# First 128 tokens ranked and gathered ahead; expert 0 begins without gates and list; first refill in halves; odd gathers around down

## Chip, cores and metric

One core of a Trainium2 chip. The metric is the device time of one execution in microseconds (us); the median of three runs of the kernel before is 1189.14 us (1188.91 to 1189.64).

## What is computed

One decoder layer in float32 for 256 tokens (S) of width 1024 (D). A front part makes one projection of x, sparse attention and a convolution branch, mixes them and adds the residual: `x1 = LayerNorm(alpha * x + mix)`. The mixture of experts follows: `logits = x1 @ w_router + b_router`, the top 4 of 32 experts per token, a softmax over the four as gates, and for each expert `act = (u + 1) * (g * sigmoid(1.702 g))` with clamped `g, u = t @ w_gate_up[e] + b_gate_up[e]`, then `out += gate * (act @ w_down[e] + b_down[e])`. A tail computes `LayerNorm(h + sigmoid(h @ W_pg) * (p @ W_pp))`.

## The kernel before

**Tiling.** Tokens stand in two blocks t of 128 (NT = 2). An expert takes its tokens in slots of CAP = 64: a one-hot matrix `sel` (token by slot, for two experts q = 0, 1 at once) gathers the rows of x1 by matmul into `XT` (8 blocks k of 128 features). `mask` says which expert a token picked (`pick`, L1546), a matmul with `upper` and `ones` counts the tokens ahead (L841 to L843), `slot1` (L1588) is the slot number, `one_hot` (L460) compares it with a ramp. Experts with more than 64 tokens take a second round: `wide` (L1596, L1600) holds that flag, which every engine loads into a register before it branches (`read_flag`, L506). Tokens beyond 128 of one expert go on a list (`need`, `place`, `more`; L861, L871), worked off behind expert 31.

**Weights.** Each expert needs six loads of 2 MB (`load_pair`, L336; CPE = 6): four for gate and up (w_gu), two for down (w_dn). There are ES = 11 places. Loads 0 to 10 are issued during the front part; from load 11 on (L560) SyncE waits until TensorE has used what lay in the place (`chunk_used`, `gu_done`, `d_done`; `pair_read`, L339) and issues the next. SyncE issues in order; transfers queue behind one another.

**An expert in one round** (`one_round`, L986) on TensorE: turn the gates by slot (`turn_gates`, L381), 32 gate-up products (L389, in two passes each, so 64 records in the trace), two turns of the result (L396), the flag, `before(e)`: the output of the expert ahead is spread to the tokens by `combine` (L409), then in odd experts the gather for the next two (L376), then down (16 products, 32 records). `use_down` (L914) waits for `t_read`, which VectorE sets when it has read both halves of the turned up-part (second L435 in `swiglu`), and for `act_ready` (L453), half by half. ScalarE evacuates the sums (L1261), the down rows (L1264) and the gathered rows (`xt_out`, L496). Expert 0 also turns the bias rows (L967), waits for ScalarE's copy (L1272) and combines them before down.

**The stretch around the change** (215 to 265 us). TensorE interleaves the last mixing products (L791) with turns of the residual (L801) and the router (L809); four short matmuls (`keep_clock`, L831) fill waits. VectorE: residual and statistics, `scale` (L1531) and `shift` (L1543) of each half row of x1, `pick(0)`, later `pick(1)`, slots of both blocks, one-hot of both, the last half of x1, the flags, the gates (L1602 to L1608), gates by slot (L472), `place`. Then TensorE gathers with both blocks, ScalarE evacuates XT, and expert 0 starts. GpSimd (POOL) has nothing to do between its bias work (L626) and two memsets (L629, L630), behind which SyncE loads the bias rows of down (L556).

## Time and profile before

| | |
|---|---|
| median of 3 runs | 1189.14 us |
| the profiled execution, its own time | 1189.43 us |
| its span, first to last instruction | 1187.7 us |
| TensorE busy | 1151.7 us (97%) |
| VectorE, ScalarE, GpSimd busy | 297.9, 172.5, 11.4 us |
| DMA moved | 448.16 MB |
| expert 0's first product starts | 239.09 us |
| experts end, tail begins | 1149.9 us |

An engine's busy time is the union of its instructions. L389 is line 389 of the kernel; helpers give all their instructions one line, so a product of any expert is L389. Times below are from the start of the span; the profiled execution takes 1.7 us more than its span.

### The profile page before, as it was taken

The numbers are of one execution on the slowest core, as the hardware profiler recorded it, in microseconds if no ns is written. First come the engines' busy times: TensorE is split into PE (matmuls) and PEld (weight loads), VectorE is DVE, ScalarE is ACT, GpSimd is POOL, SyncE is SP. The second block draws the span as 40 slices with busy tenths as digits, with TensorE's granted clock in tenths as the row PEclk, the third lists the DMA queues.
The fourth block names the chain that finished last, engine by engine and source line by source line (L and its number), as shares of the span: only waits on it lengthen the run. The fifth ranks groups of instructions, "written<-read, shape, count | busy, mean of one in ns | idle before, by whom it ended". The sixth has DMA issues, their size and how long they took to land.

```text
span 1187.7 us, 13709 instructions
## 1 busy us (share of the span) xinstructions
PE 1151.7 (97%) x5616; PEld 580.0 (49%) x5616; DVE 297.9 (25%) x769; ACT 172.5 (15%) x335; POOL 11.4 (1%) x26
## 2 busy tenths in 40 slices
PE   7999999999999999999999899999999999999997
PEld 6888888834343434434343343434344343434346
DVE  0549932611111121111110211111212111111125
ACT  1214130111010111101110110101111011111112
POOL 0020000000000000000000000000000000000000
PEclk9999999999999999999998999999999999999999
DMA  9994467689999999999999999999999999999970
GB/s 322 347 298 142 142 233 263 251 365 426 429 427 428 427 428 427 427 429 427 427 426 427 424 398 430 427 427 428 428 427 427 428 428 427 427 427 428 427 335 36
DMA packets 64887, 448.16 MB, mean 377 GB/s; under 512 B 7120, under 2 KB 36080, under 8 KB 39984
## 3 DMA queue, kind: packets, MB, share of 16 engines
q1 hardware_dynamic: 58352, 440.84, 90.1%
q10 hardware_dynamic: 6464, 6.33, 1.6%
q8 instruction: 49, 0.80, 0.3%
q14 instruction: 22, 0.18, 0.0%
HBM read 444.53 MB, written 2.62 MB: 376 GB/s over the span
## 4 chain that ended last, share of the span: by engine, by line
PE 89%; DVE 5%; DMA 4%; ACT 1%; issue 1%; ACTq 0%; DVEq 0%
PE bank L389 55%; PE bank L649 11%; PE bank L376 5%; DMA ring<-in_w_gu 3%; PE bank L409 3%; PE bank L778 2%; PE bank L791 2%; PE bank L1093 2%; PE bank L396 2%; PE bank L704 1%; DVE arena L435 1%; PE bank L383 1%; DVE arena L429 1%; ACT arena L1261 1%; DVE arena L453 1%
## 5 line engine op out<-in xcount | busy, mean ns | idle before, releaser
L389 PE MATMUL bank<-ring,arena 128*64 128x512 f32 x1712 | 377.4, 595 | 6.8 <-DVE arena L435 4.3
L389 PE MATMUL bank<-arena 128*64 128x512 f32 x1456 | 322.9, 598 | 4.8 <-DVE arena L435 3.9
L389 PEld LDWEIGHTS bank<-ring,arena 128*64 128x64 f32 x1712 | 120.2, 137 | 242.0 <-issue 225.1
L389 PEld LDWEIGHTS bank<-arena 128*64 128x64 f32 x1456 | 102.0, 138 | 208.2 <-issue 193.6
L429 DVE TENSOR_TENSOR arena<-bank,arena 128x512 f32<-128x512 f32 x33 | 22.8, 691 | 598.4 <-PE bank L396 598.4
L649 PE MATMUL bank<-arena,ring 128*128 128x256 f32 x576 | 129.3, 386 | 0.0
L649 PEld LDWEIGHTS bank<-arena,ring 128*128 128x128 f32 x576 | 111.2, 194 | 17.2 <-issue 2.1
L1261 ACT ACTIVATE arena<-bank 128x512 f32<-128x512 f32 x62 | 37.0, 597 | 395.4 <-PE bank L389 395.4
L409 PE MATMUL bank<-arena 64*128 64x512 f32 x272 | 67.6, 615 | 1.3 <-ACT arena L1264 0.8
L376 PEld LDWEIGHTS bank<-sel,arena 128*128 128x128 f32 x512 | 61.6, 197 | 12.5 <-issue 12.2
L376 PE MATMUL bank<-sel,arena 128*128 128x128 f32 x512 | 64.8, 285 | 0.7 <-DVE wide L1600 0.7
L1264 ACT ACTIVATE arena<-bank 128x512 f32<-128x512 f32 x33 | 19.7, 597 | 243.3 <-PE bank L389 238.6
L396 PEld LDWEIGHTS bank<-arena 128*128 128x128 f32 x264 | 36.7, 209 | 35.2 <-issue 25.5
L396 PE MATMUL bank<-arena 128*128 128x128 f32 x264 | 48.8, 309 | 3.3 <-ACT arena L1261 0.4
L1447 DVE SCALAR_TENSOR_TENSOR arena<-arena 128x256 f32<-128x256 f32 x120 | 48.5, 479 | 0.7 <-DVE arena L1447 0.2
L409 PEld LDWEIGHTS bank<-arena 64*128 64x128 f32 x272 | 23.5, 186 | 22.9 <-issue 17.5
L462 DVE TENSOR_TENSOR sel<-arena 128x256 f32<-128x256 f32 x16 | 6.8, 425 | 103.9 <-PE bank L383 103.9
L1159 ACT ACTIVATE arena<-bank,arena 128x256 f32<-128x256 f32 x36 | 16.8, 472 | 103.1 <-PE bank L649 103.1
L453 DVE TENSOR_TENSOR arena<-arena 128x256 f32<-128x256 f32 x66 | 28.1, 425 | 4.9 <-ACT arena L458 0.9
L449 DVE SCALAR_TENSOR_TENSOR arena<-arena 128x256 f32<-128x256 f32 x66 | 28.1, 425 | 4.4 <-DVE arena L445 0.4
L500 ACT ACTIVATE arena<-bank 128x512 f32<-128x512 f32 x32 | 19.1, 597 | 68.5 <-PE bank L376 68.5
L791 PE MATMUL bank<-ring,arena 128*128 128x256 f32 x128 | 28.4, 380 | 0.0
(198 smaller groups left out, 534.5 us busy)
## 6 DMA issues: line engine op xcount, KB each, us to landing
ring<-in_w_gu SPq DMA_DIRECT2D x70, 2048.0 KB, 25.7
arena<-in_w_gu SPq DMA_DIRECT2D x58, 2048.0 KB, 27.3
ring<-in_w_dn SPq DMA_DIRECT2D x35, 2048.0 KB, 25.8
arena<-in_w_dn SPq DMA_DIRECT2D x29, 2048.0 KB, 27.2
ring<-in_w_in SPq DMA_DIRECT2D x19, 1024.0 KB, 12.9
ring<-in_w_out SPq DMA_DIRECT2D x4, 1024.0 KB, 5.6
arena<-in_w_pg SPq DMA_DIRECT2D x2, 2048.0 KB, 44.8
ring<-in_w_oa SPq DMA_DIRECT2D x2, 1024.0 KB, 5.4
```

The lines of the kernel that those rows point to most:

```text
L376: mm = pe.matmul(bank[b + k // 4][:, (k % 4) * P:(k % 4 + 1) * P], x1_rows[:, t, k // 2, k % 2, :], sel[:, t, :, :], start=(t == 0), stop= ...
L389: mm = pe.matmul(to[half * CAP:(half + 1) * CAP, :], rows, w[:, half * 512:(half + 1) * 512], start=first, stop=last)
L396: mm = pe.transpose(to[:, j * P:(j + 1) * P], blocks[:, j, :], ident)
L409: mm = pe.matmul(total[t][n][:, :], G2[a:a + CAP, q, t * P:(t + 1) * P], ysb[a:a + CAP, :], start=first, stop=last)
L429: nc.vector.tensor_tensor(by_bias(gt, 8), by_bias(of_gate[:, :], 8), bias_of(e, 0, 0, 8), ALU.add).then_inc(sw_step, 1)
L449: nc.vector.scalar_tensor_tensor(up[:, at], up[:, at], 1.0, gt[:, at], ALU.add, ALU.mult).then_inc(sw_step, 1 + 6 * skip * j)
L453: nc.vector.tensor_tensor(to[:, at], up[:, at], sg[:, at], ALU.mult).then_inc(act_ready, 1 + 2 * skip * j)
L649: mm = pe.matmul(bank[n % 4][:, 0:S], w[:, k, j * P:(j + 1) * P], xT_sb[:, k, :], start=(k == 0), stop=(k == KD - 1))
L778: mm = pe.matmul(bank[n % 4][:, 0:S], w_view(i)[:, k, (c % 4) * P:(c % 4 + 1) * P], rhs[:, k, :], start=(k == 0), stop=(k == 3))
L791: mm = pe.matmul(mix_bank(t, j), merged[:, k, t * P:(t + 1) * P], w_view(25 + j)[:, k, :], start=(k == 0), stop=(k == KD - 1))
L1261: a.activation(rows, of[:, :], ACT.Identity).then_inc(h_out, 1 + 2 * j)
L1447: nc.vector.scalar_tensor_tensor(cy[:, a, :], u_sb[:, a, bass.ds(j, S)], dw[:, a, bass.ds(j, 1)], cy[:, a, :], ALU.mult, ALU.add).then_inc ...
```

## The change

Block t = 0 is ranked by itself as soon as its mask is there (`slots(0)`, `first_one_hot(0)`), and its part of the gather goes to banks 2 and 3 (`first_gather`), from where ScalarE copies it to XT; the part of t = 1 goes to banks 0 and 1 and VectorE adds it to XT. GpSimd does the scale of the last half row of x1, in two instructions. The flag is written as an integer at once. Expert 0's gates and the list are made inside its gate-up products (`rank_further` at k = 2, `first_gates` at k = 4, `list_further` behind k = 5), its bias turn and combine stand behind down. Load 11 is issued in two halves. `use_down` waits for `sig_in` instead of `t_read`, and in odd experts half the next gather stands before each half of down. The sigmoid table is asked for ahead of the experts. Left out here are declarations, the same edits in the path of two rounds, and the counts of `wide_ready`.

```diff
...
@@ -312,7 +313,7 @@
             last_in.append(max([m for m in range(n) if slot_no[m] == i], default=-1))
-            turn_of[i] += 1
+            turn_of[i] += 2 if n == ES else 1
             slot_no.append(i)
@@ -334,6 +335,13 @@
         def load_pair(sp, n, e, c):
+            if n == ES:
+
+                for half in range(2):
+                    at = slice(half * SLOT, (half + 1) * SLOT)
+                    sp.wait_ge(*((chunk_used, 1) if half else (half_used, 1)))
+                    sp.dma_start(slot_of(n)[:, at], pair_source(e, c)[:, at]).then_inc(e_in[slot_no[n]], 16)
+                return
             sp.dma_start(slot_of(n), pair_source(e, c)).then_inc(e_in[slot_no[n]], 16)
@@ -367,16 +375,24 @@
-        def gather(pe, b=4, first=False, ks=range(KD)):
+        def gather(pe, b=4, ks=range(KD)):
             for k in ks:
-                if first and k % 4 == 0:
-                    pe.wait_ge(x1_ready, 3 + k // 4)
                 for t in range(NT):
...
+
+        def first_gather(pe, t, ks):
+
+            for k in ks:
+                if t == 1 and k % 4 == 0:
+                    pe.wait_ge(x1_ready, 3 + k // 4)
+                mm = pe.matmul(bank[2 - 2 * t + k // 4][:, (k % 4) * P:(k % 4 + 1) * P], x1_rows[:, t, k // 2, k % 2, :],
+                               sel[:, t, :, :], start=True, stop=True)
+                if k % 4 == 3:
+                    mm.then_inc((gath_first, gath_done)[t], 1)
@@ -464,6 +480,11 @@
+        def first_one_hot(v, t, done):
+            nc.vector.tensor_tensor(sel[:, t, :, :], iota_c[:, 0:CAP].unsqueeze(1).to_broadcast([P, 2, CAP]),
+                                    slot1[:, t, 0:2].unsqueeze(2).to_broadcast([P, 2, CAP]),
+                                    ALU.is_equal).then_inc(done, 1)
+
@@ -558,7 +579,8 @@
                 for n in range(ES, NG):
-                    sp.wait_ge(*pair_read(last_in[n]))
+                    if n > ES:
+                        sp.wait_ge(*pair_read(last_in[n]))
                     if n == PP:
@@ -625,6 +647,13 @@
+
+                g.wait_ge(ln_in, 32)
+                g.wait_ge(var1, 2)
+                g.tensor_scalar(x1[:, 1, 512:D], res[:, 1, 512:D], mv[:, 1, 0:1], None, ALU.subtract
+                                ).then_inc(pool_scaled, 1)
+                g.wait_ge(pool_scaled, 1)
+                g.tensor_tensor(x1[:, 1, 512:D], x1[:, 1, 512:D], lng1[:, 512:D], ALU.mult).then_inc(pool_scaled, 1)
                 g.wait_ge(x1_ready, 4)
@@ -824,7 +853,10 @@
                 route(1, range(4))
+                pe.wait_ge(mask_ready, 1)
+                pe.matmul(bank[6][:, 0:NE], upper, mask[:, 0, 0:NE], start=True, stop=True).then_inc(cum_done, 1)
                 mix(1, 3, range(4, KD))
@@ -832,34 +864,39 @@
                 turn_res(1, 3)
-                keep_clock(1)
+                pe.wait_ge(sel_half, 1)
+                pe.matmul(bank[6][:, NE:2 * NE], ones, mask[:, 0, 0:NE], start=True, stop=False)
+                pe.wait_ge(res_ready, 8)
+                first_gather(pe, 0, range(2))
                 route(1, range(6, KD))
-                pe.wait_ge(mask_ready, 1)
-                keep_clock(3)
+                first_gather(pe, 0, range(2, KD))
                 pe.wait_ge(mask_ready, 2)
-                pe.matmul(bank[6][:, 0:NE], upper, mask[:, 0, 0:NE], start=True, stop=True)
-                pe.matmul(bank[6][:, NE:2 * NE], upper, mask[:, 1, 0:NE], start=True, stop=False)
-                pe.matmul(bank[6][:, NE:2 * NE], ones, mask[:, 0, 0:NE], start=False, stop=True).then_inc(cum_done, 1)
-
+                pe.matmul(bank[6][:, NE:2 * NE], upper, mask[:, 1, 0:NE], start=False, stop=True).then_inc(cum_done, 1)
                 for t in range(NT):
...
                     for t in range(NT):
-                        mm = pe.matmul(bank[7][j * NE:(j + 1) * NE, 0:1], mask[:, t, 0:NE], ones[:, 0:1],
+                        mm = pe.matmul(bank[5][j * NE:(j + 1) * NE, 0:1], mask[:, t, 0:NE], ones[:, 0:1],
                                        start=(t == 0), stop=(t == NT - 1))
...
                 pe.wait_ge(sel_ready, 1)
-                gather(pe, 0, True, range(4))
+                first_gather(pe, 1, range(4))
                 flag = pe.alloc_register("pe_two_rounds")
-                pe.wait_ge(wide_ready, 2)
+                pe.wait_ge(wide_ready, 1)
                 read_flag(pe, flag, 0)
-                gather(pe, 0, True, range(4, KD))
+                first_gather(pe, 1, range(4, KD))
                 pe.wait_ge(more_ready, 1)
-                pe.matmul(bank[6][0:MORE, RANK:RANK + 1], upper[0:MORE, 0:MORE], need, start=True, stop=True
-                          ).then_inc(rank_done, 1)
+
+                def rank_further():
+                    pe.matmul(bank[6][0:MORE, RANK:RANK + 1], upper[0:MORE, 0:MORE], need, start=True, stop=True
+                              ).then_inc(rank_done, 1)
+
+                def first_gates(done):
+                    pe.wait_ge(selg_ready, 1)
+                    turn_gates(pe, selg[:, 0]).then_inc(sgt_done, done)
@@ -887,11 +924,20 @@
+
+                        if wait_xt and k == 2:
+                            rank_further()
+                        if wait_xt and k == 4:
+                            first_gates(3)
                         at = slice(k % 2 * SLOT, (k % 2 + 1) * SLOT)
...
                         mm = part(k, 1, w[:, at])
+                        if wait_xt and k == 0:
+                            mm.then_inc(half_used, 1)
                         if k % 2 == 1:
                             mm.then_inc(chunk_used, 1)
+                    if wait_xt:
+                        list_further()
                     w = weights(3)
@@ -908,12 +954,16 @@
                                 mm.then_inc(gu_done, 1)
+                        if e == 0 and k == 0:
+                            mm.then_inc(half_used, 1)
                         if k in (1, 3, 5):
...
-                def use_down(e, weights):
-                    pe.wait_ge(t_read, e * 2 + 2)
+                def use_down(e, weights, done=3, gathers=False):
+                    pe.wait_ge(sig_in, e * 2 + 2)
                     for i in range(2):
+                        if gathers:
+                            next_gather(e, range(4 * i, 4 * i + 4))
                         w = weights(4 + i)
@@ -922,7 +972,7 @@
                             mm.then_inc(chunk_used, 1)
-                    mm.then_inc(d_done, 3)
+                    mm.then_inc(d_done, done)
@@ -947,19 +997,18 @@
                     pe.wait_ge(rows_out, e * 2 + 2)
-                    combine(pe, q, last=last, done=done)
-
-                def next_gather(e):
+                    return combine(pe, q, last=last, done=done)
+
+                def next_gather(e, ks=range(KD)):
                     pe.wait_ge(sel_ready, e // 2 + 2)
-                    gather(pe)
+                    gather(pe, ks=ks)
...
                         pe.wait_ge(bias_ready, 1)
-                        combine(pe, 1, first=True)
-                    else:
-                        rows_of(e - 1, 1 - e % 2)
+                        return combine(pe, 1, first=True)
+                    return rows_of(e - 1, 1 - e % 2)
@@ -986,11 +1035,10 @@
                     weights = lambda c: pair(load_no(e, c))
-                    turn_gates(pe, selg[:, q]).then_inc(sgt_done, 3)
+                    if e:
+                        turn_gates(pe, selg[:, q]).then_inc(sgt_done, 3)
                     embedded(e)
                     use_gate_up(e, q, weights, e == 0)
-                    if e == 0:
-                        list_further()
                     for j, (rows, to) in enumerate(((h_gate, gate_turned), (h_up, up_turned))):
@@ -1001,21 +1049,25 @@
                     read_flag(pe, flag, e + 1)
+                    if e:
+                        before(e)
+                    if e in (PP_E, PP_E + 2):
+                        embed(e)
+                    use_down(e, weights, 3 if e else 2, q == 1 and e < NE - 1)
                     if e == 0:
                         turn_bias(gate_sum)
-                    before(e)
-                    if q == 1 and e < NE - 1:
-                        next_gather(e)
-                    if e in (PP_E, PP_E + 2):
-                        embed(e)
-                    use_down(e, weights)
+                        before(e).then_inc(d_done, 1)
...
                     weights = lambda c: pair(load_no(e, c))
-                    turn_gates(pe, selg[:, q]).then_inc(sgt_done, 1)
+                    if e:
+                        turn_gates(pe, selg[:, q]).then_inc(sgt_done, 1)
+                    else:
+                        first_gates(1)
                     embedded(e)
                     if e == 0:
+                        rank_further()
                         list_further()
@@ -1063,7 +1115,7 @@
                             pe.wait_ge(xt_ready, e // 2 + 1)
-                        pe.wait_ge(selg_ready, e // 2 + 1)
+                            pe.wait_ge(selg_ready, e // 2 + 1)
                     pe.br_ne(flag, 0, f"pe_two_rounds{e}", f"pe_one_round{e}")
@@ -1244,7 +1296,13 @@
                 a.activation(rl[:, :, :], rl[:, :, :], ACT.Exp).then_inc(rl_exp, 1)
-                xt_out(a, 1, 0)
+                for b in range(2):
+                    a.wait_ge(gath_first, b + 1)
+                    a.activation(XT[:, 4 * b:4 * b + 4, :, :],
+                                 bank[2 + b][:, :].rearrange("p (k q c) -> p k q c", k=4, q=2), ACT.Identity
+                                 ).then_inc(xt_first, 1)
+
+                a.activation(ssum[:, 0, 0:1], epsc, ACT.Sigmoid)
@@ -1281,12 +1339,12 @@
                     sums_out(e)
-                    if e == 0:
-                        bias_out(gate_sum)
                     read_flag(a, flag, e + 1)
...
                     embedded(e)
+                    if e == 0:
+                        bias_out(gate_sum)
                     a.wait_ge(d_done, 3 * e + 3)
@@ -1575,29 +1633,43 @@
+
+                def slots(t):
+                    nc.vector.scalar_tensor_tensor(slot1[:, t, 0:NE], bank[6][:, t * NE:(t + 1) * NE], 1.0,
+                                                   mask[:, t, 0:NE], ALU.add, ALU.mult).then_inc(v_chain, 1)
+                    v.wait_ge(v_chain, c.up())
+
+                v.wait_ge(cum_done, 1)
+                v.wait_ge(mask_ready, 1)
+                slots(0)
+                first_one_hot(v, 0, sel_half)
                 residual(1, 3)
...
                 scale(1, 0)
-                one_over(1)
+                v.wait_ge(std1, 2)
+                nc.vector.reciprocal(rstd[:, 1:2], rstd[:, 1:2]).then_inc(inv1, 1)
+                v.wait_ge(inv1, 1)
                 pick(1)
...
-                v.wait_ge(cum_done, 1)
+                v.wait_ge(cum_done, 2)
                 v.wait_ge(mask_ready, 2)
-                for t in range(NT):
-                    nc.vector.scalar_tensor_tensor(slot1[:, t, 0:NE], bank[6][:, t * NE:(t + 1) * NE], 1.0,
-                                                   mask[:, t, 0:NE], ALU.add, ALU.mult).then_inc(v_chain, 1)
-                v.wait_ge(v_chain, c.up(2))
-                one_hot(v, 0)
-                scale(1, 1)
+                slots(1)
+                first_one_hot(v, 1, sel_ready)
+
+                v.wait_ge(cum_done, 3)
+                nc.vector.tensor_scalar(wide[:, :], bank[4][0:1, 0:NE], float(CAP), None, ALU.is_gt
+                                        ).then_inc(wide_ready, 1)
+                nc.vector.tensor_tensor(need, bank[5][0:MORE, 0:1], above, ALU.is_gt).then_inc(more_ready, 1)
+                v.wait_ge(pool_scaled, 2)
                 shift(1, 1)
-
-                v.wait_ge(cum_done, 2)
-                nc.vector.tensor_scalar(wide_f, bank[4][0:1, 0:NE], float(CAP), None, ALU.is_gt
-                                        ).then_inc(wide_ready, 1)
-                nc.vector.tensor_tensor(need, bank[7][0:MORE, 0:1], above, ALU.is_gt).then_inc(more_ready, 1)
-                v.wait_ge(wide_ready, 1)
-                nc.vector.tensor_copy(wide[:, :], wide_f).then_inc(wide_ready, 1)
+                for b in range(2):
+                    v.wait_ge(xt_first, b + 1)
+                    v.wait_ge(gath_done, b + 1)
+                    nc.vector.tensor_tensor(XT[:, 4 * b:4 * b + 4, :, :],
+                                            bank[b][:, :].rearrange("p (k q c) -> p k q c", k=4, q=2),
+                                            XT[:, 4 * b:4 * b + 4, :, :], ALU.add
+                                            ).then_inc(xt_half if b == 0 else xt_ready, 1)
                 v.wait_ge(rl_exp, 1)
...
```

## Rows read from the trace of the kernel before

**Rows 1.** Windows: engines busy, granted clock, DMA share, GB/s in two stretches.
```profile
245.00:621.00 376.00, 367.78 (x1804) 147.59 (x1800) 67.25 (x180) 47.49 (x85) 0.00 (x0) 1.00 1.01 427
621.35:631.59 10.24, 9.55 (x37) 6.71 (x38) 0.00 (x0) 0.98 (x2) 0.00 (x0) 0.50 1.01 424
```
**Rows 2.** Waits of PE: us in total, times, longest.
```profile
PE bank L389 <- DVE arena L435: 8.1, 14, 0.9
PE bank L383 <- issue: 1.6, 1, 1.6
```
**Rows 3.** L337, single weight loads: ns, issue time; then us from issue to landing.
```profile
L337 SPq DMA_DIRECT2D ring<-in_w_dn x1: 327/327/327, 228.3 to 228.3; - x1
L337 SPq DMA_DIRECT2D arena<-in_w_dn x1: 1292/1292/1292, 228.7 to 228.7; - x1
DMA to landing us min/median/max: 7.7/10.1/12.4
...
L337 SPq DMA_DIRECT2D ring<-in_w_dn x1: 346/346/346, 242.8 to 242.8; - x1
DMA to landing us min/median/max: 8.9/8.9/8.9
...
L337 SPq DMA_DIRECT2D arena<-in_w_dn x1: 328/328/328, 269.5 to 269.5; - x1
DMA to landing us min/median/max: 11.5/11.5/11.5
...
L337 SPq DMA_DIRECT2D ring<-in_w_dn x1: 328/328/328, 294.3 to 294.3; - x1
DMA to landing us min/median/max: 11.2/11.2/11.2
...
L337 SPq DMA_DIRECT2D ring<-in_w_dn x1: 328/328/328, 686.0 to 686.0; - x1
DMA to landing us min/median/max: 9.6/9.6/9.6
```
**Rows 4.** Timeline of PE, 236 to 266 us: start, us, line, [idle before <- releaser].
```profile
236.47 2.12 PE L376 MATMUL bank<-sel,arena 128*128 128x128 f32 x16 [0.70 <-DVE wide L1600]
...
239.09 13.95 PE L389 MATMUL bank<-ring,arena 128*64 128x512 f32 x64
...
253.56 1.21 PE L396 MATMUL bank<-arena 128*128 128x128 f32 x8 [0.35 <-DVE more L1634]
...
255.55 1.99 PE L409 MATMUL bank<-arena 64*128 64x512 f32 x8 [0.56 <-ACT arena L1272]
258.46 7.09 PE L389 MATMUL bank<-ring,arena 128*64 128x512 f32 x32 [0.92 <-DVE arena L435]
...
265.85 13.96 PE L389 MATMUL bank<-arena 128*64 128x512 f32 x64
```
**Rows 5.** Timeline of PE: expert 2 at its turns and down, and expert 31's last gate-up.
```profile
308.39 1.58 PE L396 MATMUL bank<-arena 128*128 128x128 f32 x8
...
312.44 3.65 PE L389 MATMUL bank<-ring,arena 128*64 128x512 f32 x16 [0.56 <-DVE arena L435]
...
1132.49 3.65 PE L389 MATMUL bank<-ring,arena 128*64 128x512 f32 x16 [0.99 <-DMA ring<-in_w_gu]
```
**Rows 6.** Timeline of VectorE and GpSimd.
```profile
229.55 0.75 DVE L1531 SCALAR_TENSOR_TENSOR arena<-arena 128x512 f32<-128x512 f32 x1
...
231.69 0.18 DVE L1561 TENSOR_SCALAR arena<-picked 128x32 f32<-128x32 f32 x1
...
235.14 0.74 DVE L1600 CAST wide<-arena 1x32 int32<-1x32 f32 x1
...
235.32 0.52 POOL L630 MEMSET arena<- 128x512 f32 x1
...
311.63 0.42 DVE L453 TENSOR_TENSOR arena<-arena 128x256 f32<-128x256 f32 x1
```
**Rows 7.** Groups of POOL: busy us, mean ns, idle before.
```profile
L626 POOL TENSOR_TENSOR arena<-arena 128x768 f32<-128x768 f32 x4 | 7.1, 1807 | 0.2 <-POOL arena L621 0.2
```

More of the change, by code:

```diff
@@ L194, in program @@
         iota_c = view(o + 1735, WIDE)
-        wide_f = view(o + 1863, NE)[0:1, :]
         stats4 = view(o + 1895, 48).rearrange("p (t a b) -> p t a b", t=NT, a=4)
@@ L216, in program @@
         arrived = [sem(f"slot{i}_arrived") for i in range(NS)]
-        chunk_used = sem("chunk_used")
+        chunk_used, half_used = sem("chunk_used"), sem("half_used")
         small_in, late_in = sem("small_in"), sem("late_in")
@@ L245, in program @@
         var1, std1, x1_ready = sem("var1"), sem("std1"), sem("x1_ready")
+        inv1, pool_scaled, sel_half = sem("inv1"), sem("pool_scaled"), sem("sel_half")
+        gath_first, xt_first = sem("gath_first"), sem("xt_first")
         res_ready, rt_done, rt_out = sem("res_ready"), sem("resT_done"), sem("resT_out")
@@ L1316, in two_rounds @@
                     embedded(e)
-                a.wait_ge(wide_ready, 2)
+                a.wait_ge(wide_ready, 1)
                 read_flag(a, flag, 0)
@@ L1611, in _ @@
                 v.wait_ge(v_chain, c.up())
+                v.wait_ge(sel_half, 1)
                 gates_by_slot(v, 0, 1)
@@ L1650, in two_rounds @@
                     swiglu(v, e, 1, gate_turned, up_turned, act_b, True)
-                v.wait_ge(wide_ready, 2)
+                v.wait_ge(wide_ready, 1)
                 read_flag(v, flag, 0)
```

## The prediction, made before the changed kernel was run

> **What bounds the kernel now.** I read the windows first. From 245 to 621 us TensorE is busy 367.78 of 376 us and the DMA share is 1.01 at 427 GB/s: two full resources [rows 1]. The waits of TensorE do not name the weights as the limit: its largest item is VectorE's L435, 8.1 us in 14 stops [rows 2], one in each even expert. So who sets the end? The refills answer. A load of 2,048 KB (2.097 MB) at 427 GB/s takes 4.91 us, and one that meets an empty queue lands 7.7 us after its issue [rows 1, 3]. The refill issued at 242.8 lands at 251.7, the one issued at 269.5, six loads later, at 281.0: 29.3 us, 4.89 each, so nothing is lost between them [rows 3]. The margin, landing time less 7.7, says how long a load stood behind others: 3.8 us at 269.5, 3.5 at 294.3, 1.9 at 686.0 [rows 3]. In these loads it never falls to zero, and DMA moves its full 427 GB/s throughout [rows 1], so the stream of refills is unbroken from its first load on, and its end is its start plus a constant. At 1132.49 TensorE stops 0.99 us for gate-up weights of expert 31 [rows 5]: it has eaten the lead of eleven loads, and a faster TensorE alone would wait there longer. The end is therefore set by **when the first refill lands**, as long as TensorE releases places soon enough to keep the margins.
>
> Sums go against the profiled execution's 1189.43 us; its three runs' median is 0.3 lower.
>
> **Start of expert 0.** Before, a chain on VectorE runs from L1531 (229.55) over the mask L1561 (231.69) to the flag L1600 (235.14, 0.74 us), whose reading TensorE awaits before the second half of the gather at 236.47; products begin at 239.09 [rows 4, 6].
> - Added ahead of it: one short matmul pair before the last mixing products, 0.22 us (an estimate: half the gather's 2.12 us for 16 records is 1.06 for 8, and this is 2 records of a smaller form) [rows 4]. The chain of `pick(1)` moves by +0.22, its mask from 231.69 to 231.91.
> - Taken off VectorE: the last `scale`, 0.75 us by the equal L1531, the flag's cast, and half of the one-hot, ranked early where VectorE waits for mixing anyway [rows 6]. Left behind the mask are about 1.0 us to the end of `shift`, 0.4 for slot and one-hot of t = 1; select ready near 233.35.
> - The gather of t = 1 is 16 records instead of 32, so 2.1 us instead of 4.2 [rows 4], 233.4 to 235.5. VectorE's `shift(1,1)` and flag run beside its first half. VectorE's add of the first half of XT (0.7 us, as its other 512-wide work) lies beside the second. ScalarE's copy of t = 0 is done before. Gates and rank no longer stand between gather and products. Products begin near 235.7 if nothing collides: 3.4 us earlier.
> - **The collision.** GpSimd now works from `var1` (229.8) on. Its price is not in the trace. Per instruction the ends are 0.52 us (the 128x512 memset) and 1.2 (1.81 x 512/768) [rows 6, 7]; I take 0.65 for the one with a single tensor, near the memset, and 1.2 for the other. Beside the memsets the cast on VectorE took 0.74 us for 32 numbers and ended when they did [rows 6]. If POOL begins behind L1531 (230.5) its pair ends at 232.4 to 232.7, with a step of VectorE between them. The mask, due at 231.91, would wait for it, 0.8 us; ends 0 (no collision) and 1.0. I take 0.8, since the cast is the one row of such a meeting. Products begin at 236.5: 2.6 us earlier.
>
> The Trainium skill speaks against this part (page "SBUF — State Buffer", section "Who interferes with whom"): GpSimd and VectorE lock a port pair for a whole instruction, also when a VectorE instruction has two SBUF inputs and GpSimd reads SBUF. By that rule the second step of `pick(1)` waits as well as the mask; the sum stays near 0.8, because both wait for the same pair of instructions. The cast's 0.74 agrees for the one-input case; no row here shows two inputs.
>
> **Inside expert 0.** Before, from first product to expert 1's first product: 265.85 - 239.09 = 26.8 us [rows 4]. After:
> - products 13.95 plus rank, gates and list among them, 0.8 (two transposes 0.4, three tiny pairs): 14.75
> - turns, then down as soon as `act_ready` stands. In expert 2 L453 ends at 312.05, so down could start at 312.1 instead of 312.44: 3.6 behind its gate-up [rows 5, 6]. The table load is taken out of that path
> - down 7.0
> - bias turn 0.4, ScalarE's copy 0.57 (the wait before L409), combine 1.95, expert 1's gates 0.4 [rows 4]: 3.3, uncovered now; before, this combine lay inside VectorE's time.
>
> Together 28.7: expert 0 gets 1.9 us longer. Expert 1 begins 2.6 - 1.9 = 0.7 us earlier (1.5 without collision).
>
> **The stream.** Load 11 was issued at 242.8. Its halves are now issued 1.8 and 3.6 us behind the first product, at 238.3 and 240.1, while load 10 (228.7 + 12.4 = 241.1) is landing [rows 3]. So load 11 lands at 241.1 + 4.9 = 246.0. Load 12 waits for four k and rank: 236.5 + 7.4 = 243.9, landing 251.5; before it was 251.7 + 4.9 = 256.6. The stream is 5.0 us earlier. TensorE is only 0.7 earlier, so margins shrink by the difference. At 269.5: needed 5.0 - 0.7 = 4.3, margin 3.8: 0.5 lost. At 294.3: needed 3.8, margin 3.5: 0.3 lost. **4.2 us remain** (5.0 without collision, by the same steps). The release at 290.8, expert 1's first down half, would be worse, with a margin near 2; the split gather brings it 2 us earlier and so covers it. That is all the split is worth: in odd experts no VectorE wait stands before down, and the gather takes as long in two parts.
>
> **Even experts.** `sig_in` for `t_read` saves 312.44 - 312.10 = 0.34 us in each [rows 5, 6]. Six of them lie between 1 and 14, so at 686.0 TensorE is 0.7 + 2.0 = 2.7 us earlier, the stream 4.2; needed 1.5, margin 1.9: nothing lost. At the end TensorE has gained 0.7 + 12 x 0.34 = 4.8, more than 4.2: the stream still decides. Only expert 31 lies behind its last gate-up weights, and gains its 0.35.
>
> **Sum:** 4.2 + 0.35 = 4.55; 1189.43 - 4.55 = 1184.9, at the median 1184.6. Other edits (flag as integer, table, POOL's later memset and bias loads, wanted only behind down) hide: if the bias rows' cover of about 20 us went, the first combine would wait.
>
> **Rivals.**
> 1. **The clock falls in expert 0.** TensorE started expert 14 after 1.6 us idle [rows 2], and its clock stood at 0.50 from 621.35 to 631.59 [rows 1]. Now expert 0 has 2.1 us without work between its turns and down, where a combine used to stand. For: it is longer than that stop. Against: it lies between long products, the other among short matmuls and a second stop. 10.24 us at half clock cost 5.1 us less the idle in it, 4.7. Expert 1 then begins 4.0 us later than before, the margin 3.5 at 294.3 is overdrawn by 0.5, less 0.35 gained at the end: 1189.6, at the median 1189.3, no change. In clock words 0.50 is the 1.2 GHz level, and everything else the 2.4.
> 2. **The early halves are worth nothing**, for example because two half loads land like a full one issued with the second: load 11 then lands 8.9 behind 240.1, at 249.0, a gain of 2.7, with 0.35 3.05: 1186.4, at the median 1186.1. For: a load that stands behind another never shows its own data time. Against: each half still has 8 KB in a row for each of 128 partitions, and the first is issued 1.8 us ahead.
> 3. **Slower: the clock falls twice**, ahead of the first products, where the short `keep_clock` matmuls went and TensorE waits for a mask held up by POOL, and again at expert 0's idle. It decides once expert 1 begins more than 3.5 us later than before, since that is the margin at 294.3. Price 5.1 + 4.7 = 9.8: expert 1 is 9.1 late, 5.6 over the margin, less 0.35: +5.2, 1194.4 at the median. For: that stretch is a row of short matmuls with waits. Against: the early gather fills more of it than the `keep_clock` ones did, and the present stretch, also broken, kept 1.00.
>
> **Chances.** Forecast with its collision bounds 0.60; rival 1 0.23; rival 2 0.08; rival 3 0.09. A measurement of this kernel can tell about 0.2%, 2.4 us. Faster by more: forecast and rival 2, 0.68, less 0.02 for a mixture of part costs, 0.66. Same: rival 1 and that mixture, 0.25. Slower 0.09. The predicted time is the likeliest case's, 1184.6. Its own range is 1183.2 (no collision and 0.5 of luck in the stream) to 1186.2 (rival 2 beside it). For 8 in 10 the range takes in rival 1: 1183.0 to 1189.8.
>
> **What the changed profile would show.** Right: first product of expert 0 at 236.5 (235.7 without collision); mask L1561's successor held until POOL's second instruction ends; load 12 landing near 251.5; expert 1's products from about 265.1; first down of even experts behind L453, 0.2 us idle instead of 0.56; every refill landing 4.89 us behind the last, with margins down to about zero near 269 and 294; a stop for weights in expert 31 again, near 1128. Wrong: a granted clock of 0.50 inside expert 0 (rivals 1, 3); a gap in the refills elsewhere, above all behind expert 14; a TensorE that never waits for weights at the end, which would mean that I took the wrong bound.

## The result, and the profile after

The changed kernel takes 1193.7 us (median of 8, 1192.24 to 1194.85) against 1189.39 for the kernel before on the same chips (8 runs, 1186.57 to 1191.76): a ratio of 1.0041, 95% interval 1.0031 to 1.0051. It is **slower by 0.4%**, where 0.4% faster was forecast, and outside the range. The profiled execution took 1192.24 us with a span of 1190.5, the fastest of its eight.

The two traces do not start alike: the last mixing product (L791 before, L820 after) ends at 228.29 us before and at 227.38 after. The part ahead of it is the same code but for one pair of short matmuls (L857), which puts this end back by 0.22 us: it comes 3.00 us behind the start of the router products ahead of it (224.38), and 2.78 us before (225.51). "Behind mixing" below is a time less the end of that product. It takes the drift of the front part out, and shows the changed kernel 0.22 us too early.

Expert 0 and the first refill, in the timeline of PE (columns as in rows 4), after:

```profile
233.26 2.15 PE L392 MATMUL bank<-sel,arena 128*128 128x128 f32 x16 [0.87 <-DVE sel L484]
235.42 3.65 PE L405 MATMUL bank<-ring,arena 128*64 128x512 f32 x16
...
250.49 1.57 PE L412 MATMUL bank<-arena 128*128 128x128 f32 x8
254.30 7.09 PE L405 MATMUL bank<-ring,arena 128*64 128x512 f32 x32 [2.23 <-DVE arena L469]
261.32 0.44 PE L1016 MATMUL bank<-arena 128*128 128x128 f32 x2
262.32 1.99 PE L425 MATMUL bank<-arena 64*128 64x512 f32 x8 [0.56 <-ACT arena L1330]
264.24 0.44 PE L399 MATMUL bank<-arena 128*128 128x128 f32 x2
264.61 13.95 PE L405 MATMUL bank<-arena 128*64 128x512 f32 x64
```

L405 is the product that was L389. Expert 0 begins 8.04 us behind mixing instead of 10.80 [rows 4], 2.8 earlier, or 2.5 with the added pair counted (forecast 2.6). Then 2.23 us stand empty ahead of down, and the combine follows it uncovered. Expert 1's first product is 37.23 behind mixing against 37.56: of the 2.8 us, 0.3 are left.

VectorE and GpSimd beside it, timeline after:

```profile
231.01 1.77 DVE L1601 SCALAR_TENSOR_TENSOR arena<-arena 128x512 f32<-128x512 f32 x1
...
228.79 2.04 POOL L653 TENSOR_SCALAR arena<-arena 128x512 f32<-128x512 f32 x1 [160.52 <-DVE arena L1583]
230.91 1.32 POOL L656 TENSOR_TENSOR arena<-arena 128x512 f32<-128x512 f32 x1
```

GpSimd's first instruction took 2.04 us where I had 0.65. The mask (L1619, 0.18 us) was not held; `shift(1,0)` (L1601) was: 1.77 us instead of 0.75, ending 0.55 behind GpSimd's second instruction (232.23).

The odd experts, and the stop before expert 14, timeline of PE after:

```profile
281.92 2.15 PE L382 MATMUL bank<-sel,arena 128*128 128x128 f32 x16
284.00 3.65 PE L405 MATMUL bank<-arena 128*64 128x512 f32 x16
287.58 2.15 PE L382 MATMUL bank<-sel,arena 128*128 128x128 f32 x16
289.67 3.65 PE L405 MATMUL bank<-ring,arena 128*64 128x512 f32 x16
293.25 0.44 PE L399 MATMUL bank<-arena 128*128 128x128 f32 x2
...
311.32 3.65 PE L405 MATMUL bank<-ring,arena 128*64 128x512 f32 x16 [0.32 <-DVE arena L469]
...
621.42 0.65 PE L399 MATMUL bank<-arena 128*128 128x128 f32 x2 [3.57 <-issue]
...
1155.03 5.13 PE L1145 MATMUL bank<-arena 128*128 128x256 f32 x23
```

In the kernel before the same piece reads:

```profile
283.16 4.04 PE L376 MATMUL bank<-sel,arena 128*128 128x128 f32 x32
287.12 3.65 PE L389 MATMUL bank<-arena 128*64 128x512 f32 x16
290.61 3.60 PE L389 MATMUL bank<-ring,arena 128*64 128x512 f32 x16
294.14 0.44 PE L383 MATMUL bank<-arena 128*128 128x128 f32 x2
...
619.72 0.44 PE L383 MATMUL bank<-arena 128*128 128x128 f32 x2 [1.64 <-issue]
...
1152.26 4.05 PE L1093 MATMUL bank<-arena 128*128 128x256 f32 x18
```

Gather and down take 293.25 - 281.92 = 11.33 us instead of 294.14 - 283.16 = 10.98: each split costs 0.35. Expert 2 still stops ahead of down, 0.32 us instead of 0.56, so `sig_in` gives 0.24 and not 0.34. The stop before expert 14 is 3.57 instead of 1.64 us. And the clock, windows view (columns as in rows 1), after:

```profile
621.50:635.16 13.66, 12.59 (x46) 8.54 (x48) 0.86 (x4) 0.98 (x2) 0.00 (x0) 0.50 1.01 423
635.20:1100.00 464.80, 457.81 (x2208) 183.52 (x2206) 80.16 (x210) 56.68 (x103) 0.00 (x0) 1.00 1.00 421
```

The 1.2 GHz level lasted 13.7 us instead of 10.2. Waits of PE, whole span, after:

```profile
PE bank L405 <- DVE arena L469: 8.3, 16, 2.2
PE bank L399 <- issue: 3.6, 1, 3.6
```

The list has no more waits for the experts' weights, where the kernel before had 1.2 us of them. **The bound has changed**: behind expert 14 TensorE sets the end. The refills show it, single loads after (issue time, then landing):

```profile
L345 SPq DMA_DIRECT2D ring<-in_w_gu x1: 327/327/327, 242.9 to 242.9; - x1
DMA to landing us min/median/max: 9.4/9.4/9.4
...
L345 SPq DMA_DIRECT2D ring<-in_w_gu x1: 327/327/327, 675.1 to 675.1; - x1
DMA to landing us min/median/max: 7.9/7.9/7.9
...
L345 SPq DMA_DIRECT2D ring<-in_w_dn x1: 327/327/327, 682.0 to 682.0; - x1
DMA to landing us min/median/max: 8.8/8.8/8.8
...
L345 SPq DMA_DIRECT2D ring<-in_w_dn x1: 328/328/328, 689.0 to 689.0; - x1
DMA to landing us min/median/max: 7.6/7.6/7.6
```

The loads issued at 675.1, 682.0 and 689.0 land 7.7 and 5.9 us apart (at 683.0, 690.7 and 696.6) instead of 4.9: the stream was broken behind expert 14.

Where the time went, behind mixing, in the profiled pair: expert 1's gates 0.3 us earlier; expert 14's gates at 621.42 - 227.38 = 394.04 against 391.43, 2.6 later (seven splits +2.4, six even experts -1.4, the stop +1.9, the start -0.3); expert 15's gates 457.5 against 453.7, 3.8 later, the added 1.2 in the stretch with the longer 1.2 GHz level; the tail's first product 927.65 against 923.97, 3.7 later.

### The profile page after: what moved, and what is told of

The parts are those of the page before. It is cut to its first block, busy times and chain, and to the rows that moved or that the text cites. A ratio compares the mean times of both kernels' runs of the same rounds, so it can differ in the third digit from the quotient of the medians.

```text
span 1190.5 us, 13718 instructions
## 1 busy us (share of the span) xinstructions
PE 1155.3 (97%) x5608; PEld 583.6 (49%) x5608; DVE 299.4 (25%) x770; ACT 172.5 (14%) x336; POOL 14.8 (1%) x28
## 4 chain that ended last, share of the span: by engine, by line
PE 92%; DVE 4%; issue 2%; ACT 1%; DMA 1%; SPq 0%; DVEq 0%; ACTq 0%
PE bank L405 58%; PE bank L678 10%; PE bank L382 5%; PE bank L425 3%; PE bank L807 2%; PE bank L820 2%; PE bank L1145 2%; PE bank L412 2%; PE bank L733 1%; PE bank L399 1%; DVE arena L445 1%; ACT arena L1319 1%; DMA ring<-in_w_in 1%; DVE arena L465 1%; DVE arena L469 1%
## 5 line engine op out<-in xcount | busy, mean ns | idle before, releaser
L405 PE MATMUL bank<-ring,arena 128*64 128x512 f32 x1712 | 379.7, 595 | 5.7 <-DVE arena L469 5.7
L405 PE MATMUL bank<-arena 128*64 128x512 f32 x1456 | 324.2, 598 | 3.3 <-DVE arena L469 2.6
L405 PEld LDWEIGHTS bank<-ring,arena 128*64 128x64 f32 x1712 | 122.1, 137 | 231.0 <-issue 223.8
L405 PEld LDWEIGHTS bank<-arena 128*64 128x64 f32 x1456 | 104.8, 138 | 201.4 <-issue 195.4
L382 PEld LDWEIGHTS bank<-sel,arena 128*128 128x128 f32 x480 | 58.8, 196 | 23.5 <-issue 23.5
L469 DVE TENSOR_TENSOR arena<-arena 128x256 f32<-128x256 f32 x66 | 28.1, 425 | 4.0
L820 PE MATMUL bank<-ring,arena 128*128 128x256 f32 x128 | 28.4, 380 | 0.0
```

The costliest lines, as they stand in the source:

```text
L382: mm = pe.matmul(bank[b + k // 4][:, (k % 4) * P:(k % 4 + 1) * P], x1_rows[:, t, k // 2, k % 2, :], sel[:, t, :, :], start=(t == 0), stop= ...
L405: mm = pe.matmul(to[half * CAP:(half + 1) * CAP, :], rows, w[:, half * 512:(half + 1) * 512], start=first, stop=last)
L469: nc.vector.tensor_tensor(to[:, at], up[:, at], sg[:, at], ALU.mult).then_inc(act_ready, 1 + 2 * skip * j)
L820: mm = pe.matmul(mix_bank(t, j), merged[:, k, t * P:(t + 1) * P], w_view(25 + j)[:, k, :], start=(k == 0), stop=(k == KD - 1))
```

## The experiments

The expectations speak of two theories. Theory G: the split gather made the kernel slower. Its rival E: expert 0's combine, which nothing covers now, and the front did. All times are medians; the ratio is against the kernel before on the same chip.

**1. Whole gather in the changed kernel (a_whole_gather).**

```diff
+                    if q == 1 and e < NE - 1:
+                        next_gather(e)
-                    use_down(e, weights, 3 if e else 2, q == 1 and e < NE - 1)
+                    use_down(e, weights, 3 if e else 2)
```

> The changed kernel with the whole next gather ahead of down again, all else as changed. Theory G (the split gather costs the time: 0.35 us of TensorE in each odd expert by 29.01 against 28.66 us, and a later xt_ready, so that expert 14's branch to its code of two rounds is reached 3 us later and TensorE stands 3.6 us instead of 1.6 before it): the stop before expert 14 is 1.7 us or less, odd experts take 28.7 us, a stop for weights comes back near the end, and the time is 1187 us, 2 below the kernel before and 6 below the changed one. Theory E (expert 0's bare combine and the front cost it): the stop stays 3.6 us and the time 1192 to 1194.

1189.73 us, ratio 1.0002 (0.9992 to 1.0012): 4 us come back, the stop is 1.7, and TensorE waits for weights again:

```profile
PE bank L405 <- DMA arena<-in_w_gu: 2.9, 3, 1.2
PE bank L405 <- DMA ring<-in_w_gu: 2.9, 3, 1.2
PE bank L399 <- issue: 1.7, 1, 1.7
```

So undoing the split gives back what the change lost. But 1187 was expected. The profiled execution is one of the three quickest of twelve, 1187.79 us at a mean granted clock of 0.997: its clock did not fall near expert 14. Nine others have 0.991 or 0.992 and took 1189.1 to 1191.4 us, and no trace shows where these lose it. This trace also has a fall of the clock that the changed kernel's does not, in expert 0's down:

```profile
253.52:256.93 3.41, 2.89 (x8) 1.12 (x10) 1.85 (x5) 0.00 (x0) 0.00 (x0) 0.50 0.97 413
```

**2. Expert 0's bias part ahead of down (a_bias_back)**; ScalarE's `bias_out` moves ahead of its sigmoid with it.

```diff
-                    if e:
-                        before(e)
+                    if e == 0:
+                        turn_bias(gate_sum)
+                    before(e)
...
-                    use_down(e, weights, 3 if e else 2, q == 1 and e < NE - 1)
-                    if e == 0:
-                        turn_bias(gate_sum)
-                        before(e).then_inc(d_done, 1)
+                    use_down(e, weights, 3, q == 1 and e < NE - 1)
```

> The changed kernel with expert 0's bias turn, copy and combine ahead of down, as before. Theory G: TensorE reaches expert 1 about 2 us earlier; it bounds the kernel from expert 14 on, so 2 us are gained: 1191.7. Theory E: expert 0 was the loss, all of it comes back: 1189 or less. If the stream of weights decided instead, about 2 us as well, by the later margin.

1189.69 us, ratio 1.0000 (0.9991 to 1.0009): 4 us again, where 2 were expected by G. Expert 1's gates come 34.40 us behind mixing instead of 36.86, so the traces show 2.5 of the 4; for the rest see 3.

**3. Both undone (a_whole_bias_back).** Left are the front part, the half loads, `sig_in` and the gates inside the products. As in 2, and in `one_round`:

```diff
+                    if q == 1 and e < NE - 1:
+                        next_gather(e)
...
+                    use_down(e, weights)
```

> The changed kernel with the whole gather ahead of down and expert 0's bias part ahead of down as well: of the change the front part, the half loads, sig_in and the gates inside the products are left. Theory G (split gather and late release of expert 0 cost the time): TensorE reaches expert 1 2.5 us earlier than in the changed kernel, loads keep their margins, refills land 2 us or more ahead of the kernel before, the stops for weights near the end remain: 1187, 2 below the kernel before. Rival (the end hangs on the stream alone, which nothing here moves): 1189 to 1190.

1186.17 us (12 runs), ratio 0.9978 (0.9969 to 0.9986): 3 us faster than the kernel before, 7.5 faster than the changed one. Both theories were half right: G has 4 us, the late bias part of theory E the rest. Here the combine fills the gap, timeline of PE:

```profile
250.87 1.58 PE L412 MATMUL bank<-arena 128*128 128x128 f32 x8
252.29 0.38 PE L1016 MATMUL bank<-arena 128*128 128x128 f32 x2
253.23 1.99 PE L425 MATMUL bank<-arena 64*128 64x512 f32 x8 [0.56 <-ACT arena L1330]
255.15 7.09 PE L405 MATMUL bank<-ring,arena 128*64 128x512 f32 x32
262.17 0.44 PE L399 MATMUL bank<-arena 128*128 128x128 f32 x2
```

Of the seven profiled kernels with the late bias part, six show the clock at 0.50 for 3.4 us in expert 0's down, the changed kernel being the one without; of the five variants of the changed kernel that have it ahead of down, none does. In a_whole_gather expert 0 took 30.25 us from first product to expert 1's gates, in the changed kernel 28.82: the fall costs 1.4. The changed kernel's own profile is therefore hardly its usual case: it and one more execution have a mean granted clock of 0.993 and took 1192.2 and 1192.5 us, the six others 0.991 or 0.992 and 1193.6 to 1194.9. That these six have the fall in expert 0 would explain both this and the 4 us of a_bias_back (2.5 and 1.4), but no trace of one of them shows it.

**4. The split in the kernel before (b_split_gather, b_split_sig_in).** The first, in `use_down` and `one_round`; the second has the last pair as well.

```diff
                     for i in range(2):
+                        if gathers:
+                            next_gather(e, range(4 * i, 4 * i + 4))
...
-                    if q == 1 and e < NE - 1:
-                        next_gather(e)
...
-                    use_down(e, weights)
+                    use_down(e, weights, q == 1 and e < NE - 1)
...
-                    pe.wait_ge(t_read, e * 2 + 2)
+                    pe.wait_ge(sig_in, e * 2 + 2)
```

> The kernel before with the gather split around down and nothing else. Theory G: odd experts 29.0 us instead of 28.7, stop before expert 14 3.5 us, TensorE 5 us later from the split and 2 to 4 from the stop and the clock, of which 1.2 us of former waiting for weights absorb: 1195 to 1197 us. Theory E: 1189 to 1190.

1203.45 us, ratio 1.0121 (1.0107 to 1.0136), far beyond the expectation. My edit put the gather behind the wait for `t_read`, which it had stood ahead of, so each of 15 odd experts stops; waits of PE:

```profile
PE bank L376 <- DVE arena L435: 8.5, 15, 0.8
```

> The kernel before with the split gather and sig_in in use_down, and nothing else: the price of the split without the 0.56 us stop that b_split_gather had ahead of each odd gather. Theory G: odd experts 29.0 us, even ones 25.1, a stop of about 3.5 us before expert 14, no stop for weights at the end, 1193 to 1195. If only that t_read stop made b_split_gather slow: 1189 to 1190.

1190.07 us, ratio 1.0016 (1.0007 to 1.0025). The stop before expert 14 was 3.1 us and no wait for weights was left, as expected, but the time is only 1 to 2 us more, where 4 to 6 were expected. TensorE sets the end here too, and three rows say why it comes sooner than in the changed kernel. Expert 1's gates come 36.48 us behind mixing; in the changed kernel it is 36.86, and 38.0 to 38.6 in the six traces with the fall. The stop is 0.5 us shorter. The 1.2 GHz level behind it lasts 10.2 us instead of 13.7. Without `sig_in` the same split cost some 13 us more.

**5. Where the split costs: the branch (a_branch_first, a_whole_at_13, a_split_at_13).** The wait for the gathered rows stands ahead of the branch to an expert's code; expert 14 alone jumps to the far code of two rounds, and in the two kernels of 6, which do not jump there, there is no stop. With the split the rows are ready 3.2 us later (ScalarE's second copy ends at 614.90 instead of 611.70). In a_branch_first the waits stand behind the branch, in a function at the head of both kinds of round:

```diff
-                    if e % 2 == 0:
-                        if e:
-                            pe.wait_ge(xt_ready, e // 2 + 1)
-                            pe.wait_ge(selg_ready, e // 2 + 1)
...
+                def inputs_of(e):
+                    if e and e % 2 == 0:
+                        pe.wait_ge(xt_ready, e // 2 + 1)
+                        pe.wait_ge(selg_ready, e // 2 + 1)
```

The other two, with `e != 13` (a_whole_at_13) or `e == 13` (a_split_at_13):

```diff
+                    split = e != 13
+                    if q == 1 and e < NE - 1 and not split:
+                        next_gather(e)
-                    use_down(e, weights, 3 if e else 2, q == 1 and e < NE - 1)
+                    use_down(e, weights, 3 if e else 2, q == 1 and e < NE - 1 and split)
```

> The changed kernel with the split gather, but the waits for the gathered rows and gates stand behind the branch to an expert's code, not ahead of it. Theory G: the code of two rounds is fetched while the second half of down runs, so the stop before expert 14 shrinks from 3.6 to under 0.5 us; the odd experts keep 29.0 us; time about 1189.5, 4 below the changed kernel. A rival, that the stop is a matter of longer code and not of when the branch is reached: the stop stays at 3 us or more, time 1193 to 1194. Theory E: as the changed kernel.

1193.17 us, ratio 1.0035 (1.0022 to 1.0048); the stop 2.8 us instead of 3.6. The expectation of under 0.5 failed, and the time did not clearly change. The DMA packets of 16 KB on the instruction queue tell more: in all fourteen traces of kernels with two rounds in expert 14, the one ahead of the stop's end starts about 2.5 us before it (617.20 and 619.72 before, 618.90 and 621.42 after). That packet started 0.9 us earlier against down's end here (0.17 us behind it, against 1.06) but not more, and the 16 KB packet ahead of it did not move at all: it starts 2.0 us ahead of down's end here, 1.9 in the changed kernel, 4.3 in the kernel before. So the waits for the rows are not all that holds the jump; what else does was not found. That the stop is the fetch of the far code is read from these packets.

> The changed kernel with the whole gather ahead of down in expert 13 alone; the other fourteen odd experts keep the split. Theory L (what the split costs is the late release of the branch before expert 14): the stop before expert 14 is 1.7 us instead of 3.6, and 2 to 3 of the 4 us come back: 1191. Theory S (it is the 0.35 us of each split, before and behind expert 14): stop shorter, but the time stays within 1 us of 1193.7.

1190.99 us, ratio 1.0017 (1.0008 to 1.0026), stop 2.2 us: one split of fifteen undone gives 2.7 us back. By the traces 1.35 of it lie in the stop and 1.4 in expert 14, where the 1.2 GHz level lasts 10.2 us again and not 13.7.

> The changed kernel with the split gather in expert 13 alone, whole in the other fourteen. Theory L: stop before expert 14 3.6 us, 1192 to 1193. Theory S: near a_whole_gather, 1190.

1192.08 us, ratio 1.0023 (1.0011 to 1.0035), stop 3.1 us: one split alone costs 2.4 of the 4 us, against a_whole_gather. So the larger part of the loss comes from the split at expert 13, as theory L says, and the splits elsewhere bear the rest. The mechanism of theory L, the late release of the branch, is shown only for the 0.8 us of a_branch_first.

**6. Without expert 14's second round (a_one_round, b_one_round)**: its tokens beyond 64 are left out.

```diff
-                nc.vector.tensor_scalar(wide[:, :], bank[4][0:1, 0:NE], float(CAP), None, ALU.is_gt
+                nc.vector.tensor_scalar(wide[:, :], bank[4][0:1, 0:NE], float(2 * S), None, ALU.is_gt
```

> The changed kernel without the second round of expert 14 (its tokens beyond 64 are left out), so that no far code is fetched and the lead is never refilled. Theory G: weights bound it, the split gather hides behind them, and it is 1 to 2 us faster than the same cut of the kernel before. If the loss of the change were in expert 0 or the front: 3 us or more slower than that.

> The kernel before without the second round of expert 14 (tokens beyond 64 left out). If its end is set by the stream of weights, TensorE's 35 us less work change next to nothing: 1187 to 1189. If TensorE sets it: 1160 or less.

1186.93 and 1187.30 us, ratios 0.9980 (0.9972 to 0.9989) and 0.9986 (0.9977 to 0.9995). In b_one_round TensorE reaches expert 15 39 us earlier than in the kernel before (414.6 us behind mixing against 453.7), waits 31.8 us for weights in all, and the time gains 2: **the end does hang on the stream**, as the prediction said. There the change is level with the kernel before, not 1 to 2 us faster.

**7. GpSimd's scale (a_no_pool, and w_no_pool on the version of 3)**: GpSimd's two instructions are out.

```diff
                 first_one_hot(v, 1, sel_ready)
+                scale(1, 1)
...
-                v.wait_ge(pool_scaled, 2)
                 shift(1, 1)
```

> The changed kernel with the last scale on VectorE again. By the trace of the changed kernel shift(1,0) took 1.77 us beside GpSimd's second instruction instead of 0.75, and the scale costs 0.75 on VectorE: the first product comes within 0.4 us of where it was, either side; shift(1,0) is back at 0.75. Time as the changed kernel, 1193 to 1194. If GpSimd's work cost the loss: 1191 or less.

1193.25 us, ratio 1.0037 (1.0022 to 1.0051). VectorE, timeline:

```profile
231.27 0.75 DVE L1595 SCALAR_TENSOR_TENSOR arena<-arena 128x512 f32<-128x512 f32 x1
```

`shift(1,0)` is back at 0.75 and the first product comes 7.47 us behind mixing instead of 8.04: handing the scale to GpSimd made the start 0.6 us later. It does not reach the end.

> The best version so far (a_whole_bias_back) with the last scale on VectorE instead of GpSimd. First product 0.5 us earlier, as in a_no_pool (7.47 against 8.04 us behind the last mixing product). If the stream's start sets the end: load 12 lands up to 0.5 earlier and the time is 1185.7; if load 10's landing holds load 11: 1186.2, as without.

1185.88 us, ratio 0.9977 (0.9968 to 0.9986), against 0.9978: within the measurement.

**8. Load 11 in one piece (w_full_load), on the version of 3.**

```diff
-            if n == ES:
+            if False:
...
-            turn_of[i] += 2 if n == ES else 1
+            turn_of[i] += 1
...
-                    if n > ES:
-                        sp.wait_ge(*pair_read(last_in[n]))
+                    sp.wait_ge(*pair_read(last_in[n]))
```

> The best version so far with load 11 in one piece, issued when both halves of its place are free. Theory G with the stream as the bound: load 11 issued 1.7 us later than its first half was, the stream 1 to 2 us later at its start, the time 1187 to 1188. Rival 2 of the prediction (the halves are worth nothing): 1186.2, no change.

1186.12 us, ratio 0.9981 (0.9972 to 0.9990). Rival 2 of the prediction had this part right: the halves are worth nothing. The load behind expert 0's first down half, in w_full_load and then in a_whole_bias_back:

```profile
L345 SPq DMA_DIRECT2D ring<-in_w_gu x1: 327/327/327, 258.8 to 258.8; - x1
DMA to landing us min/median/max: 9.4/9.4/9.4
```

```profile
L345 SPq DMA_DIRECT2D ring<-in_w_gu x1: 327/327/327, 258.8 to 258.8; - x1
DMA to landing us min/median/max: 9.2/9.2/9.2
```

Load 12 lands 24.7 us behind mixing with halves, and 25.8 without. But the load shown is issued at 258.8 either way, as soon as TensorE lets it, and lands at 268.2 and 268.1: the lead is given back.

**9. `t_read` again (w_t_read), on the version of 3.**

```diff
-                    pe.wait_ge(sig_in, e * 2 + 2)
+                    pe.wait_ge(t_read, e * 2 + 2)
```

> The best version so far with use_down waiting for t_read again. TensorE loses 0.24 us in each even expert (0.56 idle against 0.32), some 3 us in all, but waits for weights near the end, so theory G expects 0.3 to 1 us: 1186.5 to 1187.2. If TensorE were the bound: 1189.

1187.45 us (11 runs, 1186.34 to 1189.49), ratio 0.9992 (0.9981 to 1.0002), against 0.9978: `sig_in` is worth about 1.3 us here, more than the 0.3 to 1 expected, though the two intervals overlap. Its profile is of one of its quickest executions, at a mean granted clock of 0.998 without a fall near expert 14, and shows the stream as in 3; where the others, at 0.992 to 0.996 for the most part, lose it is open.

## Why the prediction was wrong

- **Bound before: right.** The stream of refills set the end (6). What I missed is that it did so with only 1.2 us of waiting to spare, and that the change would hand the end to TensorE. The check "TensorE has gained 0.7 + 12 x 0.34 = 4.8, more than 4.2" had every term off: 0.3 in place of 0.7, 0.24 in place of 0.34, and nothing for the splits, which cost 0.35 each.
- **Start of expert 0: right by number** (2.8 against 2.6), wrong inside. GpSimd held `shift(1,0)`, not the mask, and its first instruction took 2.04 us, above my end of 1.2. The page of the Trainium skill "SBUF — State Buffer", section "Who interferes with whom", named this case, an instruction with two SBUF inputs against a GpSimd one that reads; 1.77 instead of 0.75 us agrees. The second step of `pick(1)` (L1610) also has two SBUF inputs and by that rule should have waited for GpSimd's first instruction, which ran all around it; it took 0.25 us as ever. The mask ran in 0.18 us and met that instruction only at its end. The reason is not shown.
- **Inside expert 0: size right** (28.7 forecast to expert 1's first product, 29.2 measured, 30.6 to 30.9 with the fall of the clock), but its worth was missed. I let the margins absorb it; undone, it gives 4 us.
- **"That is all the split is worth: the gather takes as long in two parts." This step failed.** Each split costs 0.35 us. The splits together lengthen the stop before expert 14 by 1.9, and the 1.2 GHz level behind it by 3.4 us; the one at expert 13 bears most of this. My sum has no term for either. I had the row of that stop in hand and read it only for the clock. Undoing the split gives 4 us. Why the stop gets longer is shown in part only (5).
- **Even experts: over-sized.** 0.24 us each instead of 0.34. Down waits for `act_ready` and starts 0.15 us behind the end of the instruction that sets it (L469, 311.17), where I had it start at once.
- **The stream: over-sized.** 5.0 us at load 12 was forecast, 28.26 - 24.89 = 3.4 measured: load 11's second half lands 6.0 us behind load 10 instead of 4.9, and load 12 lands 9.4 us after its issue, 5.8 behind load 11, where I had 7.7 from issue. My own rows warned of it: the load at 242.8, issued when all before it had landed, took 8.9 us [rows 3]. Loads of 2 MB issued when at most 2 us of the one before was left took from 7.5 to 9.0 us in these traces, and what decides is not shown, so a margin got by taking off 7.7 can be over 1 us too large. Of the 3.4 us only 1.4 are left at load 24 (issued at 300.7, landed 85.6 us behind mixing against 87.0 before), after gaps at expert 0's and 1's releases; I had 4.2 left.
- **Rival 1 (the clock falls in expert 0): right in kind**, seen in six of seven kernels, for 3.4 us and 1.4 us of cost, not 10.24 and 4.7. **Rival 3** gave the right sign and nearly the time, 1194.4, by luck: its first fall, ahead of the first products, is in no trace.

## What to carry to other kernels

Where two resources are both near full, work out what each edit does to both all the way to the end, and do not spend margins to the last microsecond: here they were read over 1 us too large. Look for the one iteration that is not like the others: what is moved ahead of its jump to far code costs there (2.4 to 2.7 us here), even if it costs 0.35 in every other iteration. Independent work belongs into a gap that a dependency leaves, as the combine ahead of down; taken out to start sooner, it costs its full time behind the gap, and the clock may fall in the gap.

## What the runs showed of the hardware

- GpSimd's fp32 `tensor_scalar` on 128x512 took 2.04 us and `tensor_tensor` 1.32. In every trace the first began while VectorE's `scale(1,0)`, with two SBUF inputs, had 0.6 us to go, so a wait may be in the 2.04; which form is the slower by itself is not shown.
- Switching between 128-column gathers and 512-column products on TensorE cost 0.35 us for two more switches.
- TensorE stood 1.6 to 3.6 us before the jump of expert 14, and went on 2.5 us after the start of a 16 KB packet on the instruction queue, in all fourteen traces.
- Stops of about the same length behaved unlike: 2.2 us in expert 0 led to 3.4 us at the 1.2 GHz level in six of seven kernels, 1.6 us before expert 14 to 10.2 us in the kernel before, and in a_whole_gather and w_t_read, after 1.7 us there, to none. The kernel before spreads over 1186.4 to 1192.1 us, with mean clocks from 0.992 to 0.999; how much of the spread is the clock is not shown.
